# Weight-stationary matmuls taken over two weight units at a time, in a two-layer hybrid decoder trunk

## The chip, the cores and the metric

The kernel runs on one core of a Trainium2 chip. The metric is the device time of one launch in microseconds (us). Before the change it is 2441.62 us, the median of three runs (2441.19 to 2441.79). Everything below is read from one profiled execution of 2441.05 us.

## The reference, cut to what matters

The trunk has two layers on 256 tokens of width 2048, all in float32. One layer, shortened:

```
h = x @ w_in                       # 2048 -> 8336 columns: q, k, v of four head groups, and the indexer
m = concat(diff_attention x2, stick_breaking_attention, sparse_attention(indexer top-64)) @ w_out
x = layer_norm(ALPHA * x + m)
x = layer_norm(ALPHA * x + square(relu(x @ w_up)) @ w_down)     # w_up 2048 x 8192, w_down 8192 x 2048
```

Nearly all arithmetic is `activation @ weight` with 256 tokens. The sparse head group also needs a score from 16 indexer heads, summed head by head, and the 64 largest scores of each row.

## The kernel before

**Split operands.** Each float32 weight and activation is split into a rounded part (`hi`) and a remainder (`lo`), both in a reduced matmul format, and a product is the sum of hi·hi, hi·lo and lo·hi. For weights the split is made in the kernel: ScalarE (ACT) writes `hi` (line 800, `split_hi`), VectorE (DVE) writes `lo` = raw − hi (line 1048, `split_lo`).

**Chunks and units.** The weights are read in chunks of 512 output columns by 2048 rows; there are 53 a layer, numbered here from 0 in each layer: 0 the sparse group's values, 1 the indexer's keys and weights (a narrow chunk of 144 columns), 2 to 5 the indexer's queries, 6 to 16 queries, keys and values of the four groups, 17 to 20 `w_out`, 21 to 52 the MLP in four quarters of up and down chunks. A chunk consists of eight units of 256 rows, two 128-row slices each. The ring of split units (`w_hi`, `w_lo`) holds four units, so unit u of a chunk takes the place of unit u − 4, and the first four of a chunk that of units 4 to 7 of the chunk before.

**Two kinds of chunk.** In a "token" chunk the activations are TensorE's stationary operand and the weights stream by, 512 columns each (`token_tile`, lines 504 to 506). In a "feature" chunk the weights are stationary: for each of the four 128-column groups of the chunk, each with a PSUM bank of its own (n = 0 to 3), the `hi` weights meet hi and lo of the activations at once (512 columns, line 485), and the `lo` weights meet the hi activations (256 columns, line 489). There are 27 feature chunks a layer: 2 to 9, 11, 12, 14, 15, 22 to 24, and four in each of the other three quarters of the MLP.

**What sets the order.** All of it is written out by hand, and each engine runs its own list in order. TensorE (PE) waits before a unit for `lo_ready`, and before the first use of a bank in a chunk for `bank_free`. After a unit it signals `unit_free` (after the last unit `bank_full` of each bank), and `split_hi` waits for that (`before_unit` says which). ACT and DVE do their other work at fixed places between the splits: `copy_halves` and `add_halves` or `take_hidden` (the results of the chunk before) after unit 1; `index_add` (eight DVE instructions, line 1235) and, in chunk 8, `logits` after unit 6 and before unit 7; `top_k_round` after unit 7 of chunk 6 and after units 0 to 6 of chunk 7; in chunk 22 `turned_hidden_hi` (line 818) and `turned_hidden_lo` after units 6 and 7; in chunk 23 `residual_offset` (line 1135) after each unit. PE's own other work stands after a given unit too: `index_logits` after unit 1, `turn_probs`, `attend` and `turn_rows` after units 0, 2 and 4, and in chunk 22 `turn_hidden` (line 558) after units 4 and 5.

Of the kernel before, what the change touches and what calls it, by code (L numbers as in the profile page):

```python
# [23 lines left out]
PAIR = 2  # L24
# [15 lines left out]
def build(nc, x, w_in, w_out, lam_vecs, a_norm_g, b_norm_g, c_norm_g, idx_k_norm_g, idx_k_norm_b,  # L40
          ln1_g, ln1_b, w_up, w_down, ln2_g, ln2_b, rel_bias, out):
    _, SEQ, D = x.shape
# [11 lines left out]
    UNITS = KT // PAIR  # L54
    TT = SEQ // P
    HC = COLS // P
# [77 lines left out]
    with ExitStack() as ctx:  # L134
        def sb(name, shape, dt=F32):
            return ctx.enter_context(nc.sbuf_tensor(name, shape, dt))

        def sem(name):
            return ctx.enter_context(nc.semaphore(name))
# [4 lines left out]
        act_a = sb("act_a", [P, KT, 2, SEQ], F32R)  # L144
# [39 lines left out]
        pw = ctx.enter_context(nc.psum_tensor("pw", [P, HC, COLS], F32))  # L184
# [28 lines left out]
        lo_ready = sem("lo_ready")  # L213
        unit_free = sem("unit_free")
# [85 lines left out]
        def unit_home(c, u, lo):  # L300
            if CLOSING[c] and u < RING:
                return act_a[:, LOAD * u + PAIR * lo:LOAD * u + PAIR * (lo + 1)].rearrange("p k a t -> p k (a t)")
            slot = u % RING
            if OPENING[c]:
                where, slot, _ = OPEN_HOME[u]
                if where == "park":
                    return park[:, PAIR * lo:PAIR * (lo + 1)]
                if where == "act_b":
                    return act_b[:, LOAD * slot + PAIR * lo:LOAD * slot + PAIR * (lo + 1)].rearrange("p k a t -> p k (a t)")
            if c % NC == IKW:  # L310

                return w_hi[:, slot * PAIR:(slot + 1) * PAIR, lo * KW:(lo + 1) * KW]
            return (w_lo if lo else w_hi)[:, slot * PAIR:(slot + 1) * PAIR, 0:WIDTH[c]]

        def unit_hi(c, u):
            return unit_home(c, u, 0)

        def unit_lo(c, u):
            return unit_home(c, u, 1)
# [147 lines left out]
        def _(pe):  # L467

            def wait_bank(c, b):

                if USES[c][b] > 0:
                    pe.wait_ge(bank_free[b], USES[c][b])

            def feature_unit(c, u):

                hi, lo = unit_hi(c, u), unit_lo(c, u)
                pe.wait_ge(lo_ready, c * UNITS + u + 1)
                for n, b in enumerate(BANKS[c]):
                    if u == 0:

                        wait_bank(c, b)
                    cols = slice(n * P, (n + 1) * P)
                    for i in range(PAIR):
                        k = PAIR * u + i
                        nc.tensor.matmul(pw[:, b, :], hi[:, i, cols], act_a[:, k].rearrange("p a t -> p (a t)"),  # L485
                                         start=(k == 0), stop=False)
                    for i in range(PAIR):
                        k = PAIR * u + i
                        last = nc.tensor.matmul(pw[:, b, SEQ:2 * SEQ], lo[:, i, cols], act_a[:, k, 0, :],  # L489
                                                start=False, stop=(k == KT - 1))  # L490
                    if u == UNITS - 1:
                        last.then_inc(bank_full[b], 1)
                if u < UNITS - 1:
                    last.then_inc(unit_free, 1)

            def token_tile(c, u, t, src):
# [200 lines left out]
            def mixer(layer):  # L697
                for lc in range(MLP0):
# [7 lines left out]
                    for u in range(UNITS):  # L706
# [5 lines left out]
                        if KIND[c] == "feature":  # L712
                            feature_unit(c, u)
                        elif c == 0:
                            pe.wait_ge(lo_ready, u + 1)
                            for t in range(TT):
                                token_tile(c, u, t, act_a)
                                if u == 0:
                                    turn_x(0, t, 1)
                        elif lc == IKW:  # L720
                            ikw_unit(c, u)
                        else:
                            token_unit(c, u, act_a if lc < OUT0 else act_b)
# [22 lines left out]
            def mlp(layer):  # L746
                for quarter in range(QUARTERS):
                    for j in range(Q_CHUNKS):
                        c = layer * NC + MLP0 + quarter * Q_CHUNKS + j
                        if OPENING[c]:  # L750
                            open_block(c, 2 * layer + 1)
                            continue
                        if CLOSING[c]:
                            close_block(c, 2 * layer + 2)
                            continue
                        for u in range(UNITS):
                            if j < UPS:
                                feature_unit(c, u)
                                if (quarter, j) == (0, 1) and 4 <= u < 4 + TT:
                                    turn_hidden(layer, u - 4)  # L760
                                continue
                            if j == UPS:

                                pe.wait_ge(b_ready, hidden_count(layer, quarter, PAIR * u + 1))
                            token_unit(c, u, act_b)
# [797 lines left out]
```

## Time and profile before

| what | value |
|---|---|
| median of three runs | 2441.62 us |
| profiled execution | 2441.05 us, its span 2439.3 us |
| PE busy | 2419.4 us, 99% of the span |
| weight loads (PEld) busy | 2062.8 us, 85% |
| DVE busy | 1496.7 us, 61% |
| ACT busy | 1123.7 us, 46% |
| feature matmuls of 512 columns (line 485) | 3456, 33% of the chain that ended last |
| feature matmuls of 256 columns (line 489) | 3456, 16% of that chain |
| PE's share of that chain | 97% |
| mean granted clock of TensorE | 0.998 of full speed |

The first table of the page gives how long each engine was busy. Matmuls overlap their neighbours in it (a 512-column matmul is shown with 397 ns, while the next one starts some 230 ns later), so what a matmul costs is read from the distance between starts. The chain that ended last is followed back from the last instruction, at each step to what released it. Its 97% on PE says that the other engines seldom hold PE up.

### The profile page before, as it was taken

How to read it: one execution, taken by the hardware profiler on the slowest of the kernel's cores; microseconds unless marked ns; L12 is line 12 of the kernel's file. 1: busy time of each engine (PE TensorE's matmuls, PEld its weight loads, DVE VectorE, ACT ScalarE, POOL GpSimd, SP SyncE). 2: the span in 40 equal slices, each digit the busy share in tenths (PEclk: the TensorE clock that was granted, in tenths of full speed). 3: DMA queues.
4: the chain of work that ended last, by engine and by line, in shares of the span. 5: the costliest groups of instructions: out<-in, count | busy, mean ns of one | idle time of the engine just before them, and what ended most of it. 6: DMA issues, size and time to landing. Idle time of an engine off the chain costs nothing.

```text
span 2439.3 us, 30052 instructions
## 1 busy us (share of the span) xinstructions
PE 2419.4 (99%) x12557; PEld 2062.8 (85%) x12557; DVE 1496.7 (61%) x2068; ACT 1123.7 (46%) x1558; POOL 25.5 (1%) x60
## 2 busy tenths in 40 slices
PE   9999999999999999999999999999999999999998
PEld 8888888888888888888888888888888888888886
DVE  5576666667556556566675766666775655665566
ACT  4445444445345344344454444443553443443443
POOL 2000000000000000000000000000000000000001
PEclk9999999999999999999999999999999999999999
DMA  8555555646655555655555555546466565555553
GB/s 306 173 172 173 173 171 168 231 156 207 223 191 189 191 190 190 194 188 187 195 170 173 173 173 172 166 164 240 141 235 194 175 206 190 189 191 190 191 191 119
DMA packets 229752, 457.98 MB, mean 188 GB/s; under 512 B 7456, under 2 KB 12368, under 8 KB 228464
## 3 DMA queue, kind: packets, MB, share of 16 engines
q1 hardware_dynamic: 228000, 444.91, 55.6%
q0 software_dynamic: 1616, 11.14, 1.2%
q8 instruction: 99, 1.62, 0.3%
q14 instruction: 37, 0.30, 0.0%
HBM read 452.35 MB, written 3.67 MB: 187 GB/s over the span
## 4 chain that ended last, share of the span: by engine, by line
PE 97%; DVE 1%; ACT 1%; DMA 0%; issue 0%; SPq 0%; DVEq 0%; ACTq 0%
PE pw L485 33%; PE pw L489 16%; PE pw L504 14%; PE pw L506 14%; PE pw L505 14%; PE pa L583 1%; PE pa L659 1%; PE pa L580 1%; PE pa L550 0%; ACT w_hi L800 0%; PE pw L521 0%; DMA y<-in_x_dram 0%; DVE w_lo L1048 0%; PE pa L667 0%; PE pa L637 0%
## 5 line engine op out<-in xcount | busy, mean ns | idle before, releaser
L1048 DVE TENSOR_TENSOR w_lo<-raw,w_hi 128x1024 fp32r<-128x1024 f32 x804 | 971.1, 1223 | 653.0 <-ACT w_hi L800 645.4
L800 ACT ACTIVATE w_hi<-raw 128x1024 fp32r<-128x1024 f32 (+1 forms) x820 | 847.6, 1046 | 974.2 <-PE pw L506 509.2
L485 PE MATMUL pw<-act_a,w_hi 128*128 128x512 f32 x3456 | 1090.6, 397 | 3.9 <-DVE v_r L1088 3.3
L489 PEld LDWEIGHTS pw<-act_a,w_lo 128*128 128x128 f32 x3456 | 649.2, 188 | 153.2
L489 PE MATMUL pw<-act_a,w_lo 128*128 128x256 f32 x3456 | 679.2, 278 | 0.0
L485 PEld LDWEIGHTS pw<-act_a,w_hi 128*128 128x128 f32 x3456 | 528.0, 189 | 6.8 <-DVE v_r L1088 3.7
L504 PE MATMUL pw<-w_hi,act_b 128*128 128x512 f32 x1216 | 474.3, 390 | 0.1
L506 PE MATMUL pw<-w_hi,act_b 128*128 128x512 f32 x1216 | 473.2, 389 | 0.0
L505 PE MATMUL pw<-w_lo,act_b 128*128 128x512 f32 x1216 | 473.1, 389 | 0.0
L504 PEld LDWEIGHTS pw<-w_hi,act_b 128*128 128x128 f32 x1216 | 228.2, 188 | 47.7 <-DVE act_b L1331 0.9
L506 PEld LDWEIGHTS pw<-w_hi,act_b 128*128 128x128 f32 x1216 | 228.2, 188 | 47.5
L505 PEld LDWEIGHTS pw<-w_lo,act_b 128*128 128x128 f32 x1216 | 228.3, 188 | 46.7
L807 ACT ACTIVATE half<-pw 128x256 f32<-128x256 f32 x216 | 83.0, 384 | 177.4 <-PE pw L489 177.4
L504 PE MATMUL pw<-w_hi,act_a 128*128 128x512 f32 x272 | 108.7, 400 | 1.9 <-DVE w_lo L1048 1.9
L506 PE MATMUL pw<-w_hi,act_a 128*128 128x512 f32 x272 | 106.0, 390 | 0.0
L505 PE MATMUL pw<-w_lo,act_a 128*128 128x512 f32 x272 | 106.0, 390 | 0.0
L1072 DVE TENSOR_TENSOR k_t<-pw,half 128x256 f32<-128x256 f32 x120 | 50.2, 418 | 44.3 <-ACT half L807 44.3
L1109 DVE TENSOR_TENSOR y<-y,pw 128x512 f32<-128x512 f32 x48 | 33.0, 687 | 61.9 <-PE pw L506 61.9
L504 PEld LDWEIGHTS pw<-w_hi,act_a 128*128 128x128 f32 x272 | 51.1, 188 | 13.6 <-issue 3.8
L506 PEld LDWEIGHTS pw<-w_hi,act_a 128*128 128x128 f32 x272 | 51.1, 188 | 10.9
L505 PEld LDWEIGHTS pw<-w_lo,act_a 128*128 128x128 f32 x272 | 51.1, 188 | 10.5 <-issue 0.5
L1074 DVE SCALAR_TENSOR_TENSOR k_t<-k_t 128x256 f32<-128x256 f32 x120 | 51.0, 425 | 4.1
(172 smaller groups left out, 1147.8 us busy)
## 6 DMA issues: line engine op xcount, KB each, us to landing
raw<-in_w_up_dram SPq DMA_DIRECT2D x128, 1024.0 KB, 5.3
raw<-in_w_down_dram SPq DMA_DIRECT2D x128, 1024.0 KB, 5.2
raw<-in_w_in_dram SPq DMA_DIRECT2D x124, 1024.0 KB, 5.1
raw<-in_w_out_dram SPq DMA_DIRECT2D x32, 1024.0 KB, 5.1
raw<-in_w_in_dram SPq DMA_DIRECT2D x8, 512.0 KB, 10.9
work<-in_ln_g_dram POOLq DMA_DIRECT2D x4, 1024.0 KB, 6.1
work<-in_ln_b_dram POOLq DMA_DIRECT2D x4, 1024.0 KB, 8.3
raw<-in_w_in_dram SPq DMA_DIRECT2D x8, 288.0 KB, 3.9
```

The source lines that it names most:

```text
L485: nc.tensor.matmul(pw[:, b, :], hi[:, i, cols], act_a[:, k].rearrange("p a t -> p (a t)"), start=(k == 0), stop=False)
L489: last = nc.tensor.matmul(pw[:, b, SEQ:2 * SEQ], lo[:, i, cols], act_a[:, k, 0, :], start=False, stop=(k == KT - 1))
L504: nc.tensor.matmul(pw[:, b, 0:width], x_hi, hi[:, i, :], start=(k == 0), stop=False)
L505: nc.tensor.matmul(pw[:, b, 0:width], x_hi, lo[:, i, :], start=False, stop=False)
L506: last = nc.tensor.matmul(pw[:, b, 0:width], x_lo, hi[:, i, :], start=False, stop=(k == KT - 1))
L580: last = nc.tensor.matmul(pa[:, 0, h * P:(h + 1) * P], q_t[:, h, 0:P], keys(h)[:, 0:P], start=True, stop=True)
L800: nc.scalar.activation(unit_hi(c, u), raw[:, PAIR * u:PAIR * (u + 1), 0:WIDTH[c]], ACT.Copy) \
L807: nc.scalar.activation(half[:, n, :], pw[:, b, SEQ:2 * SEQ], ACT.Copy).then_inc(half_copied, 1)
L1048: V.tensor_tensor(unit_lo(c, u), raw[:, PAIR * u:PAIR * (u + 1), 0:WIDTH[c]], unit_hi(c, u).bitcast(F32), ALU.subtract).then_inc(lo_ready, 1)
L1072: V.tensor_tensor(hidden[:, n, :], pw[:, b, 0:SEQ], half[:, n, :], ALU.add).then_inc(bank_free[b], 1)
L1074: V.scalar_tensor_tensor(out=hidden[:, n, :], in0=hidden[:, n, :], scalar=0.0, in1=hidden[:, n, :], op0=ALU.max, op1=ALU.mult).then_inc(hi ...
L1109: V.tensor_tensor(piece, piece, pw[:, b, :], ALU.add).then_inc(bank_free[b], 1)
```

## The change

Only `feature_unit` changes. For odd units it returns at once; for an even unit u it waits until u and u + 1 are both split, and then runs, bank by bank, four 512-column matmuls (two slices of u, two of u + 1) and four 256-column ones. Unit u is given back after its last matmul in the last bank, unit u + 1 at the end of the pair. Work of PE that stood after an even unit now stands after the pair. No instruction is added or taken away, and the lists of ACT, DVE, SP and POOL keep their order.

```
             def feature_unit(c, u):
-                hi, lo = unit_hi(c, u), unit_lo(c, u)
-                pe.wait_ge(lo_ready, c * UNITS + u + 1)
+                if u % 2 == 1:
+                    return
+                pe.wait_ge(lo_ready, c * UNITS + u + 2)
+                pairs = [(v, i) for v in (u, u + 1) for i in range(PAIR)]
                 for n, b in enumerate(BANKS[c]):
                     if u == 0:
                         wait_bank(c, b)
                     cols = slice(n * P, (n + 1) * P)
-                    for i in range(PAIR):
-                        k = PAIR * u + i
-                        nc.tensor.matmul(pw[:, b, :], hi[:, i, cols], act_a[:, k].rearrange("p a t -> p (a t)"),
+                    for v, i in pairs:
+                        k = PAIR * v + i
+                        nc.tensor.matmul(pw[:, b, :], unit_hi(c, v)[:, i, cols], act_a[:, k].rearrange("p a t -> p (a t)"),
                                          start=(k == 0), stop=False)
-                    for i in range(PAIR):
-                        k = PAIR * u + i
-                        last = nc.tensor.matmul(pw[:, b, SEQ:2 * SEQ], lo[:, i, cols], act_a[:, k, 0, :],
+                    for v, i in pairs:
+                        k = PAIR * v + i
+                        last = nc.tensor.matmul(pw[:, b, SEQ:2 * SEQ], unit_lo(c, v)[:, i, cols], act_a[:, k, 0, :],
                                                 start=False, stop=(k == KT - 1))
-                    if u == UNITS - 1:
+                        if n == HC - 1 and v == u and i == PAIR - 1:
+                            last.then_inc(unit_free, 1)
+                    if u == UNITS - 2:
                         last.then_inc(bank_full[b], 1)
-                if u < UNITS - 1:
+                if u < UNITS - 2:
                     last.then_inc(unit_free, 1)
```

On PE, chunk 4 (indexer queries), from the last bank of unit 1 to unit 2; `pa<-k_idx_t,q_t` are the index logits. Before:

```order
L485 MATMUL pw<-act_a,w_hi 128x512 x2
L489 MATMUL pw<-act_a,w_lo 128x256 x2
L580 MATMUL pa<-k_idx_t,q_t 128x128 [waits idx_relu,bank_free3]
L580 MATMUL pa<-k_idx_t,q_t 128x128 x3
L583 MATMUL pa<-k_idx_t,q_t 128x256 x4
L485 MATMUL pw<-act_a,w_hi 128x512 [waits lo_ready]
L485 MATMUL pw<-act_a,w_hi 128x512
L489 MATMUL pw<-act_a,w_lo 128x256 x2
L485 MATMUL pw<-act_a,w_hi 128x512 x2
L489 MATMUL pw<-act_a,w_lo 128x256 x2
```

The same place in the changed kernel (its lines are two to four higher):

```order
L487 MATMUL pw<-act_a,w_hi 128x512 x3
L491 MATMUL pw<-act_a,w_lo 128x256 x4
L584 MATMUL pa<-k_idx_t,q_t 128x128 [waits idx_relu,bank_free3]
L584 MATMUL pa<-k_idx_t,q_t 128x128 x3
L587 MATMUL pa<-k_idx_t,q_t 128x256 x4
L487 MATMUL pw<-act_a,w_hi 128x512 [waits lo_ready]
L487 MATMUL pw<-act_a,w_hi 128x512 x3
L491 MATMUL pw<-act_a,w_lo 128x256 x4
L487 MATMUL pw<-act_a,w_hi 128x512 x4
L491 MATMUL pw<-act_a,w_lo 128x256 x4
```

The logits stay behind unit 1. The one wait behind them now is for units 2 and 3 together, and 32 matmuls follow before the next wait instead of 16.

On PE, chunk 22 (the second up chunk of the MLP), around the two transposes of the first chunk's rows, `pa<-ident,v_r`. Before:

```order
L489 MATMUL pw<-act_a,w_lo 128x256 x2
L558 MATMUL pa<-ident,v_r 128x128 [waits rows_relu]
L558 MATMUL pa<-ident,v_r 128x128 x3
L485 MATMUL pw<-act_a,w_hi 128x512 [waits lo_ready]
L485 MATMUL pw<-act_a,w_hi 128x512
L489 MATMUL pw<-act_a,w_lo 128x256 x2
L485 MATMUL pw<-act_a,w_hi 128x512 x2
L489 MATMUL pw<-act_a,w_lo 128x256 x2
L485 MATMUL pw<-act_a,w_hi 128x512 x2
L489 MATMUL pw<-act_a,w_lo 128x256 x2
L485 MATMUL pw<-act_a,w_hi 128x512 x2
L489 MATMUL pw<-act_a,w_lo 128x256 x2
```

And now:

```order
L491 MATMUL pw<-act_a,w_lo 128x256 x4
L562 MATMUL pa<-ident,v_r 128x128 [waits rows_relu]
L562 MATMUL pa<-ident,v_r 128x128 x3
L562 MATMUL pa<-ident,v_r 128x128 [waits rows_relu]
L562 MATMUL pa<-ident,v_r 128x128 x3
L487 MATMUL pw<-act_a,w_hi 128x512 [waits lo_ready]
L487 MATMUL pw<-act_a,w_hi 128x512 x3
L491 MATMUL pw<-act_a,w_lo 128x256 x4
```

The first transpose moved from behind unit 4 to behind unit 5, and both stand together ahead of the last pair.

## Rows read from the trace of the kernel before

**Rows 1.** Timeline, PE, steady stretch of chunk 23: start us, us, engine, line, operation, count.
```profile
563.36 0.63 PE L485 MATMUL pw<-act_a,w_hi 128*128 128x512 f32 x2
563.83 0.39 PE L489 MATMUL pw<-act_a,w_lo 128*128 128x256 f32 x2
...
568.93 0.63 PE L485 MATMUL pw<-act_a,w_hi 128*128 128x512 f32 x2
```

**Rows 2.** Timeline, PE, a token chunk; 21 matmuls lie between these two starts.
```profile
1000.39 0.39 PE L504 MATMUL pw<-w_hi,act_b 128*128 128x512 f32 x1
...
1005.15 0.39 PE L504 MATMUL pw<-w_hi,act_b 128*128 128x512 f32 x1
```

**Rows 3.** Timeline, PE, chunk 1 (narrow); 8 matmuls lie between these two starts.
```profile
40.12 0.34 PE L521 MATMUL pw<-w_hi,act_a 128*128 128x288 f32 x1
...
41.09 0.34 PE L521 MATMUL pw<-w_hi,act_a 128*128 128x288 f32 x1
```

**Rows 4.** Timeline, PE, chunk 6: starts of units 3, 4 and 6.
```profile
152.63 0.63 PE L485 MATMUL pw<-act_a,w_hi 128*128 128x512 f32 x2
...
155.42 0.63 PE L485 MATMUL pw<-act_a,w_hi 128*128 128x512 f32 x2
...
160.99 0.63 PE L485 MATMUL pw<-act_a,w_hi 128*128 128x512 f32 x2
```

**Rows 5.** Timeline, ACT, chunk 6: split_hi of unit 6; in brackets idle before, and releaser.
```profile
152.89 1.06 ACT L800 ACTIVATE w_hi<-raw 128x1024 fp32r<-128x1024 f32 x1 [1.82 <-PE pw L489]
```

**Rows 6.** Timeline, DVE: index_add and split_lo of unit 7, chunk 6; unit 3, chunk 7.
```profile
155.13 3.59 DVE L1235 SCALAR_TENSOR_TENSOR score<-work,ikw,score 128x128 f32<-128x128 f32 x8
158.76 1.23 DVE L1048 TENSOR_TENSOR w_lo<-raw,w_hi 128x1024 fp32r<-128x1024 f32 x1
...
171.53 1.23 DVE L1048 TENSOR_TENSOR w_lo<-raw,w_hi 128x1024 fp32r<-128x1024 f32 x1
```

**Rows 7.** Timeline, PE: chunk 22's start, its fourth bank, transpose; chunk 23's start.
```profile
532.83 0.61 PE L485 MATMUL pw<-act_a,w_hi 128*128 128x512 f32 x2
...
536.73 0.73 PE L485 MATMUL pw<-act_a,w_hi 128*128 128x512 f32 x2 [1.65 <-DVE v_r L1088]
...
548.68 0.60 PE L558 MATMUL pa<-ident,v_r 128*128 128x128 f32 x4
...
558.17 0.70 PE L485 MATMUL pw<-act_a,w_hi 128*128 128x512 f32 x2
```

**Rows 8.** Timeline, DVE: unit 7 of chunk 22; chunk 23's first take-up and unit 3.
```profile
550.90 1.22 DVE L1048 TENSOR_TENSOR w_lo<-raw,w_hi 128x1024 fp32r<-128x1024 f32 x1 [0.26 <-ACT w_hi L800]
...
557.61 0.41 DVE L1072 TENSOR_TENSOR k_t<-pw,half 128x256 f32<-128x256 f32 x1
...
564.05 1.22 DVE L1048 TENSOR_TENSOR w_lo<-raw,w_hi 128x1024 fp32r<-128x1024 f32 x1
```

**Rows 9.** Timeline, ACT, chunk 22: split_hi of unit 7, behind the transposed rows.
```profile
549.81 1.05 ACT L800 ACTIVATE w_hi<-raw 128x1024 fp32r<-128x1024 f32 x1
```

**Rows 10.** Timeline, DVE, first layer: units 0 and 1 of chunk 2.
```profile
42.20 2.36 DVE L1048 TENSOR_TENSOR w_lo<-raw,w_hi 128x1024 fp32r<-128x1024 f32 x2 [1.19 <-ACT w_hi L800]
```

**Rows 11.** Timeline, PE: chunk 2's start, first layer; its third bank, second layer.
```profile
43.77 0.67 PE L485 MATMUL pw<-act_a,w_hi 128*128 128x512 f32 x2
...
1254.90 0.74 PE L485 MATMUL pw<-act_a,w_hi 128*128 128x512 f32 x2 [0.41 <-DVE ikw L1199]
```

**Rows 12.** Timeline, PE: the start of chunk 24.
```profile
580.78 0.63 PE L485 MATMUL pw<-act_a,w_hi 128*128 128x512 f32 x2
```

**Rows 13.** Timeline, DVE: units 2 to 5 of chunk 24.
```profile
584.00 4.87 DVE L1048 TENSOR_TENSOR w_lo<-raw,w_hi 128x1024 fp32r<-128x1024 f32 x4
```

**Rows 14.** Windows: from, to, us, busy of each engine (count), PEclk, DMA share, GB/s.
```profile
534.00:537.00 3.00, 1.35 (x8) 1.06 (x7) 2.57 (x4) 0.10 (x1) 0.00 (x0) 1.00 0.74 255
```

**Rows 15.** Timeline, PE: the warming matmuls at the kernel's start.
```profile
1.13 4.13 PE L769 MATMUL pa<-ones 128*128 128x128 f32 x18 [1.13 <-DVE ones L1518]
...
6.18 2.17 PE L769 MATMUL pa<-ones 128*128 128x128 f32 x18
```

## The prediction, made before the changed kernel had run

> **What bounds the kernel now.** I read the busy shares first (PE 99%, DVE 61%), then the chain that ended last (97% PE), then PE's timeline chunk by chunk, and for each feature chunk when the lo part of a unit was ready against when PE started that unit. The kernel is bound by PE's stream of matmuls; other engines hold it up in a few places only. So two questions decide the change: does the new order make the stream denser, and are the weights still split in time?
>
> **The matmuls themselves.** Before, four matmuls (512, 512, 256, 256 columns) come round every (568.93 − 563.36) / 8 = 0.696 us [rows 1]: the two wide ones take 0.47 us from start to start, 0.233 each, the two narrow ones the remaining 0.23, 0.115 each. A unit is 4 banks of this, 2.79 us, a pair 5.57. In a token chunk, where all are 512 wide, one takes (1005.15 − 1000.39) / 21 = 0.227 us [rows 2]. At the granted 2.4 GHz 512 columns are 0.213 us, so a matmul costs 0.013 us over its columns there; four at that rate would be 1536 columns, 0.640 + 4 × 0.0134 = 0.694 us. Only 0.003 us of 0.696 is left that switching between widths could cost. The change halves the switches in 54 chunks × 16 groups of eight: at most 0.003 × 864 = 2.3 us gained. On the other side a longer run of narrow matmuls could be held by the weight loads: the nearest row is the narrow chunk, (41.09 − 40.12) / 8 = 0.121 us for each load and its matmul [rows 3], and four of those with four at 0.227 make 1.392 a group, as now. I take 1 us gained, between 2.3 gained and, for records I may misread by 0.002 a group, 2 lost.
>
> A rule bears on how far single steps can be trusted: the Trainium skill (Perfetto Trace Analysis, section "Per-instruction lifecycle: what the profiler-reported window actually captures") says that a matmul's reported start is the start of its operand prefetch, and its end an estimate. By it 0.233 and 0.115 are no separate prices and only their sum counts, which is how I use them; who takes them as prices gets the first rival below.
>
> **What the pair does to the splits.** Two things, both against the kernel. PE now needs the odd unit when it starts the even one, 2.79 us sooner. And the even unit is given back two 256-column matmuls before the pair's end instead of one unit earlier: later by 2.79 − 0.23 = 2.56 us. The unit four places on is split later by as much, and the odd one behind it in DVE's list too, if DVE has work between them. Such an odd unit loses 2.79 + 2.56 = 5.35 us of slack. Where nothing lies between, it is enough: the split of a pair takes about 3.7 us from its release (0.26 until ACT starts, as between 152.63 and 152.89 [rows 4, 5], hi 1.06, lo twice 1.23) and PE has 5.57. The cover is gone in these places.
>
> *Chunks 3, 4, 5, 6 (index_add) and 8 (logits), in both layers.* In chunk 6 unit 2 ended at 152.63, hi of unit 6 started at 152.89 [rows 4, 5], index_add ran from 155.13 for 3.59 us, and lo of unit 7 ended at 158.76 + 1.23 = 159.99 [rows 6]; PE wanted it at 163.78, so 3.79 us remained. After: 159.99 + 2.56 = 162.55, and 0.05 until PE starts; PE wants units 6 and 7 at the end of unit 5, 160.99 [rows 4]. Stall 1.61 us. A matmul group behind a wait takes 0.10 us longer (0.73 against 0.63 in the x2 rows [rows 1, 7]): 1.71. The other four look the same to 0.02 us; in chunk 8 the logits' three instructions stand in for index_add. 5 × 1.71 = 8.55 us a layer. ACT is not what binds: index_relu ends before unit 6 is split.
>
> *Chunk 7.* DVE does a top-k round after each split, so a unit takes 2.57 us and nothing catches up. The chain is tied to the last bank of chunk 6, i.e. to the start of chunk 7 (160.99 + 5.58 = 166.57), in both orders. Lo of unit 3 ended at 171.53 + 1.23 = 172.76 [rows 6], 6.19 in; the pair wants it at 5.57. Stall 0.62 + 0.05 + 0.10 = 0.77 us. Later units of it have over 0.4 us left.
>
> *Chunk 2.* Its start now waits for unit 1 as well: lo ended at 42.20 + 2.36 = 44.56 [rows 10], PE had started at 43.77 [rows 11]: + 0.84 with the 0.05. But four waits for banks in its unit 0 go, since each bank is now asked for 1.39 us apart: 0.29 us in the first layer and 0.89 in the second, whose largest is the wait for ikw (0.41 shown idle, more with the slow group behind [rows 11]). Net + 0.55 and − 0.05.
>
> *Chunk 22.* The fourth bank was asked for at 2.09 us and came at 536.73 − 532.83 = 3.90 [rows 7]; now it is asked for at 4.18, so the 1.82 us stall goes and 0.10 with it; the wait of 0.24 at its end goes too. What is late next is unit 7: ACT first takes the transposed rows, which PE now makes after unit 5, not 4. The transpose starts at 6 × 2.79 = 16.72; lo of unit 7 ended 550.90 + 1.22 − 548.68 = 3.44 after it [rows 7, 8], with hi of unit 7 at + 1.13 [rows 9]. So 20.16, PE at 20.21, the pair ends at 20.21 + 0.10 + 5.57 = 25.88. Before, the chunk took 558.17 − 532.83 = 25.34 [rows 7]: + 0.54. PE idles 2.7 us there.
>
> *Chunk 23.* DVE's residual_offset stands after each split. From lo of unit 7 of chunk 22 (20.16) it does 0.6 + 1.1 + 0.6 + 1.1 + 0.6 us and starts the take-up at 24.2; from there to the end of unit 3 it is 564.05 + 1.22 − 557.61 = 7.66 [rows 8], so 31.84, or 5.96 into the chunk against 5.57 wanted: stall 0.39 + 0.15. The old bank waits of this chunk, 0.32, go: + 0.2.
>
> *Other up chunks (22 boundaries to check).* Chunk 24 starts at 580.78 [rows 12]; lo of units 2 and 3 ended at 584.00 + 4.87 / 2 = 586.44 [rows 13], 5.66 in, where 5.57 is wanted. But the hidden rows' take-up was late because DVE needs 0.80 us a bank and banks filled every 0.70; now they fill every 1.39, and the last one's chain ends 0.3 us sooner: 5.3 to 5.4. I count no stall; if I am wrong by 0.2 on the 21 to 22 such places it costs 4 us.
>
> **Sum.** First layer 8.55 + 0.77 + 0.55 + 0.54 + 0.2 = 10.6, second 10.0, the stream − 1: + 19.6 us on the profiled execution's 2441.05, 2460.7; the median of the runs is 0.57 above that execution, so 2461.2.
>
> **Rivals.** (a) *The stream gets denser and pays for it.* If wide matmuls among their own kind run at the token chunk's 0.227 [rows 2], while the narrow ones keep 0.115 [rows 1], a group of eight takes 1.368 instead of 1.393: 864 × 0.025 = 21.6 us, and the time is 2439, a little faster than before. For it: the wide steps do read 0.233 next to narrow ones. Against: it needs a matmul to cost 0.013 over its columns when wide and 0.008 when narrow, and the narrow chunk's 0.121 a load [rows 3] speaks for slower, not faster. It decides once the gain passes 20.6 us.
> (b) *The narrow run is held by its loads on top:* narrow steps of 0.121 with wide ones left at 0.233, 864 × 4 × 0.006 = 21 us more, 2482. The same two rows, read the other way.
> (c) *Half of the stalls are not there*, since DVE's or ACT's lists slip less than I count (another release, an earlier hi): 2451.
> (d) *The clock falls in the new pauses.* At the start 18 small matmuls took 4.13 us, later 2.17 [rows 15]: the lower level (1.2 GHz) for about that stretch costs 2 us. With 16 pauses that is up to 32 us, 2493. The stretch with the 1.65 us pause kept 1.00 granted [rows 14], and only chunk 22's pause is longer. The Trainium skill (TensorE: Matmul & The Clock Gate, section "HAM oscillation — how this bites in real kernels") says that pauses between bursts can bring the engine back to half clock; no row before the change shows it, and I give it little: if at chunk 22 alone, 4 us more.
>
> **Chances.** Forecast 0.77, (a) 0.06, (b) 0.04, (c) 0.08, (d) 0.05. The likeliest time is 2461, its own range 2456 to 2467 (the up chunks' 4 us, the stream's 2.3 and − 2, 0.2 a stall). The range for 8 in 10 is 2453 to 2468. A change of 0.2%, 4.9 us, is about what a measurement can tell from none: slower 0.93; (a) splits into 0.03 faster and 0.04 same, with a sliver of (c).
>
> **What would show it.** In the profile after, PE should wait for DVE w_lo at the start of the fourth pair of chunks 3 to 6 and 8 by about 1.5 us idle each, ten times, at the second pair of chunk 7 by 0.5, and at the fourth of chunk 22 by 2.5; the wait for v_r should be gone. Four wide and four narrow matmuls should come round every 1.39 us. If that reads 1.37, (a) is right; 1.41, (b); if the waits for w_lo come to less than 10 us, my account of the splits is wrong.

## The result and the profile after

| | before | after |
|---|---|---|
| median of the runs | 2441.68 us | 2470.98 us (2470.77 to 2472.13) |
| ratio of the runs | | 1.0122, 95% interval 1.011 to 1.0134 |
| span of the profiled execution | 2439.3 us | 2470.3 us |
| mean granted clock of TensorE | 0.998 | 0.997 |

The change costs 29.3 us in the medians, 31.0 from profile to profile (the profiled execution after, 2472.13 us, is the slowest of its runs). Forecast were 2461 and a range of 2453 to 2468: the direction was right, the size 10 us short, and the time lies outside the range.

The page after: the span, the busy times, and the engines' shares of the chain that ended last.

```profile
span 2470.3 us, 30052 instructions
...
PE 2432.3 (98%) x12557; PEld 2073.7 (84%) x12557; DVE 1485.4 (60%) x2068; ACT 1103.1 (45%) x1558; POOL 25.5 (1%) x60
...
PE 93%; DVE 4%; ACT 2%; issue 1%; DMA 0%; DVEq 0%; ACTq 0%
```

PE left 4 points of the chain to DVE and ACT. Its busy time rose by 13 us for the same 12557 matmuls, so waits are not all of it. PE's waits, as engine, line, what released it, total us, times, longest:

```profile
PE pw L487 <- DVE w_lo L1052: 21.5, 18, 2.5
```

Of line 485 before, the page had waits for `v_r`, 3.3 us in two, and for `ikw`, 0.4 in one. Both are gone and 18 waits for split weights stand in their place: five by 1.39 us in each layer (chunks 3 to 6 and 8), 0.69 at chunk 2, 0.48 in chunk 7, 2.45 in chunk 22, 0.18 in chunk 23. Here is the first kind on PE's timeline, chunk 4's last pair, and behind it DVE's list over the same stretch:

```profile
113.47 0.64 PE L491 MATMUL pw<-act_a,w_lo 128*128 128x256 f32 x4
115.49 1.19 PE L487 MATMUL pw<-act_a,w_hi 128*128 128x512 f32 x4 [1.39 <-DVE w_lo L1052]
```

```profile
109.45 1.23 DVE L1052 TENSOR_TENSOR w_lo<-raw,w_hi 128x1024 fp32r<-128x1024 f32 x1 [5.86 <-ACT w_hi L804]
110.59 3.59 DVE L1239 SCALAR_TENSOR_TENSOR score<-work,ikw,score 128x128 f32<-128x128 f32 x8
114.22 3.50 DVE L1052 TENSOR_TENSOR w_lo<-raw,w_hi 128x1024 fp32r<-128x1024 f32 x3
```

Unit 6 is split, then the eight instructions of index_add run, and only then comes unit 7, done at 114.22 + 1.23 = 115.45. PE had been free since 114.1 and starts at 115.49. The 5.86 us ahead of unit 6 are DVE's wait for a unit that PE now gives back late. Before, it was 4.24 us:

```profile
104.16 1.23 DVE L1048 TENSOR_TENSOR w_lo<-raw,w_hi 128x1024 fp32r<-128x1024 f32 x1 [4.24 <-ACT w_hi L800]
```

That is 12.33 us into chunk 4 (which then started at 91.83), and now it is 14.95 us in (94.50): later by 2.62, where the prediction has 2.56.

The steady stream, chunk 24 [rows 1]:

```profile
597.19 1.09 PE L487 MATMUL pw<-act_a,w_hi 128*128 128x512 f32 x4
...
599.99 1.09 PE L487 MATMUL pw<-act_a,w_hi 128*128 128x512 f32 x4
600.92 0.64 PE L491 MATMUL pw<-act_a,w_lo 128*128 128x256 f32 x4
601.40 1.09 PE L487 MATMUL pw<-act_a,w_hi 128*128 128x512 f32 x4
...
605.61 1.09 PE L487 MATMUL pw<-act_a,w_hi 128*128 128x512 f32 x4
```

Six groups of eight lie between the first start and the last: (605.61 − 597.19) / 6 = 1.403 us, where two groups of four took 1.393.

Chunk 22, from its two transposes to the last pair [rows 7], then windows over it (from, to, us, busy of each engine with count, granted clock, DMA share, GB/s) [rows 14]:

```profile
560.93 1.03 PE L562 MATMUL pa<-ident,v_r 128*128 128x128 f32 x8
564.42 2.08 PE L487 MATMUL pw<-act_a,w_hi 128*128 128x512 f32 x4 [2.45 <-DVE w_lo L1052]
566.30 1.05 PE L491 MATMUL pw<-act_a,w_lo 128*128 128x256 f32 x4
```

```profile
562.00:564.00 2.00, 0.00 (x0) 0.00 (x0) 1.55 (x2) 2.00 (x4) 0.00 (x0) 1.00 0.00 0
564.00:566.00 2.00, 1.58 (x4) 1.29 (x5) 2.00 (x3) 1.49 (x2) 0.00 (x0) 0.51 0.27 44
566.00:568.00 2.00, 2.00 (x10) 1.77 (x9) 2.00 (x4) 0.39 (x1) 0.00 (x0) 0.64 0.95 307
568.00:570.00 2.00, 2.00 (x14) 1.79 (x13) 1.85 (x5) 0.39 (x1) 0.00 (x0) 1.00 0.95 278
```

Behind the pause the first four wide matmuls take 2.08 us instead of 1.09: the clock is at its lower level (1.2 of 2.4 GHz) for about 3.4 us (2.0 in the window at 0.51 and 1.4 in the one at 0.64), and the last pair takes 7.07 us until chunk 23 starts, where pair_two_two, below, takes 5.69 at full clock. The second layer does the same, with 7.26 us. That makes 2.9 us.

### The profile page after: what moved, and what is told of

It reads as the page before. It is cut to its first block, busy times and chain, and to the rows that moved or that the text cites. A ratio compares the mean times of both kernels' runs of the same rounds, so it can differ in the third digit from the quotient of the medians.

```text
span 2470.3 us, 30052 instructions
## 1 busy us (share of the span) xinstructions
PE 2432.3 (98%) x12557; PEld 2073.7 (84%) x12557; DVE 1485.4 (60%) x2068; ACT 1103.1 (45%) x1558; POOL 25.5 (1%) x60
## 4 chain that ended last, share of the span: by engine, by line
PE 93%; DVE 4%; ACT 2%; issue 1%; DMA 0%; DVEq 0%; ACTq 0%
PE pw L487 31%; PE pw L491 15%; PE pw L508 14%; PE pw L510 14%; PE pw L509 14%; DVE w_lo L1052 2%; DVE score L1239 1%; ACT w_hi L804 1%; PE pa L587 1%; PE pa L663 1%; PE pa L584 1%; PE pa L554 0%; PE pw L525 0%; PE pa L671 0%; PE pa L641 0%
## 5 line engine op out<-in xcount | busy, mean ns | idle before, releaser
L804 ACT ACTIVATE w_hi<-raw 128x1024 fp32r<-128x1024 f32 (+1 forms) x820 | 834.9, 1043 | 1058.0 <-PE pw L491 540.5
L487 PE MATMUL pw<-act_a,w_hi 128*128 128x512 f32 x3456 | 950.5, 397 | 21.5 <-DVE w_lo L1052 21.5
L487 PEld LDWEIGHTS pw<-act_a,w_hi 128*128 128x128 f32 x3456 | 593.6, 189 | 105.7 <-DVE w_lo L1052 25.2
L491 PEld LDWEIGHTS pw<-act_a,w_lo 128*128 128x128 f32 x3456 | 530.9, 189 | 73.9
L491 PE MATMUL pw<-act_a,w_lo 128*128 128x256 f32 x3456 | 550.3, 281 | 0.0
L510 PEld LDWEIGHTS pw<-w_hi,act_a 128*128 128x128 f32 x272 | 51.1, 188 | 10.9
## 6 DMA issues: line engine op xcount, KB each, us to landing
raw<-in_w_in_dram SPq DMA_DIRECT2D x8, 512.0 KB, 10.9
```

Of the source, the lines that this page charges most:

```text
L487: nc.tensor.matmul(pw[:, b, :], unit_hi(c, v)[:, i, cols], act_a[:, k].rearrange("p a t -> p (a t)"), start=(k == 0), stop=False)
L491: last = nc.tensor.matmul(pw[:, b, SEQ:2 * SEQ], unit_lo(c, v)[:, i, cols], act_a[:, k, 0, :], start=False, stop=(k == KT - 1))
L510: last = nc.tensor.matmul(pw[:, b, 0:width], x_lo, hi[:, i, :], start=False, stop=(k == KT - 1))
L804: nc.scalar.activation(unit_hi(c, u), raw[:, PAIR * u:PAIR * (u + 1), 0:WIDTH[c]], ACT.Copy) \
```

## The experiments

Open after the result: whether the 1.403 comes from the runs of four or from the pairs; whether sooner need and later release explain the waits; what the pause in chunk 22 costs. On the stream I held two theories against each other: N, a narrow matmul (256 columns) costs more straight behind another narrow one than behind a wide one (512 columns); and R, runs of four of one width cost more than runs of two. The expectations quoted below give each its numbers.

**alt_single and alt_pair.** Wide and narrow alternate one by one; in the kernel before, and inside the pairs of the changed one.

```
                     for i in range(PAIR):
                         ...                            # wide matmul of slice i
-                    for i in range(PAIR):
-                        k = PAIR * u + i
                         last = ...                     # narrow matmul of slice i
```

> The kernel before, unit by unit, but inside a bank the order is wide, narrow, wide, narrow (512, 256, 512, 256 columns). Theory N (a narrow matmul straight behind a narrow one costs about 0.009 us more than one behind a wide one; this explains 0.697 us per four before and 1.402 us per eight after): the four now take 0.688 us, 1728 times 0.009 = 15 us less, so about 2426 us. Rival S (every switch of width costs): four switches instead of two, 0.699 us or more per four, 2445 us or more. Rival F (fixed prices, the pair's slower rate comes from something else): 0.697 us, 2442 us.

> The changed kernel, pairs of units, but wide and narrow alternate slice by slice. Theory N: eight take 1.376 us instead of 1.402, 864 times 0.026 = 22 us less than the changed kernel, with the same waits for w_lo (they grow a little, as PE runs ahead faster): about 2450 us. Rival S: 1.41 us per eight or more, 2475 us or more. Rival F: 2471 us.

Measured: alt_single 2452.18 us, ratio 1.0045 (1.003 to 1.006); alt_pair 2470.80, 1.012 (1.0105 to 1.0135). PE's timeline of alt_single:

```profile
589.85 0.39 PE L485 MATMUL pw<-act_a,w_hi 128*128 128x512 f32 x1
...
591.93 0.39 PE L485 MATMUL pw<-act_a,w_hi 128*128 128x512 f32 x1
...
938.21 0.40 PE L485 MATMUL pw<-act_a,w_hi 128*128 128x512 f32 x1
...
940.33 0.40 PE L485 MATMUL pw<-act_a,w_hi 128*128 128x512 f32 x1
```

Six couples of a wide and a narrow matmul lie between the first two rows, and six between the last two: 2.08 and 2.12 us, or 0.693 and 0.707 us per four. The list of instructions is the same; the stream has two rates, and jumps between them only where something interrupts it (a transpose, a wait). Of 338 undisturbed units in this trace 57 run at the one and 281 at the other, and in alt_pair some 47 and 264. The better one beats every other order seen here, the worse one is the worst.

alt_single adds no wait and loses 10.9 us; the mean over its units, 0.7045 against 0.6977, gives 0.0068 × 1728 = 11.8. So the order of widths counts at an equal number of matmuls. The 0.688 that theory N gave isn't there: the better rate comes near it, but most units run at the worse one, above the kernel before. And one rate for one length of run, as theory R has it, is too simple as well. Rival S's numbers came for alt_single (0.699 us or more, 2445 us or more), but S can't be the rule: the changed kernel and snake, below, have fewer switches than the kernel before and a slower stream. In alt_pair, with 16.7 us of waits in 17 places where the changed kernel has 21.5 in 18, alternating makes no difference to the changed kernel's time; a slower stream waits less, so this time alone says little about the order.

**early_need.** The kernel before, but an even unit waits for the odd one too.

```
-                pe.wait_ge(lo_ready, c * UNITS + u + 1)
+                if u % 2 == 0:
+                    pe.wait_ge(lo_ready, c * UNITS + u + 2)
```

> The kernel before with its own order of matmuls and its own releases; only the wait moves: before an even unit PE waits for that unit and the next. Theory of the splits: no wait in chunks 3 to 6 and 8 (3.8 us of slack less 2.8), waits at the start of chunk 2 (0.8), at unit 2 of chunk 7 (0.7), of chunk 23 (1.3) and some 0.1 at the other up chunks: about 4 us a layer, 2450 us. Rival (needing the odd unit early is the whole cost): 16 us or more, 2458 us or more.

2450.34 us (2450.22 to 2450.84), 1.0038 (1.0023 to 1.0052), with

```profile
PE pw L486 <- DVE w_lo L1049: 4.6, 6, 1.1
PE pw L486 <- DVE v_r L1089: 3.3, 2, 1.7
```

As expected: needing the odd unit 2.79 us sooner costs 9.1 us alone. In each layer it is 0.8 us in chunk 7, 1.4 in chunk 23, 0.85 at the start of chunk 2 (of which its unit 0 gives back 0.2 and 0.8), and 0.18 to 0.20 in each of ten other up chunks. These last are the places where the prediction worked out 5.66 against 5.57 wanted and then counted nothing, since with pairs the banks fill more slowly; here they fill as before, and the wait is there. None of the ten waits of 1.39 us is there. The wait for `v_r` stays, since the banks are still asked for 0.7 us apart.

**late_release.** early_need, and units are given back as late as the pair does.

```
+                    if u % 2 == 1 and n == HC - 1:     # behind its last wide matmul, for u - 1
+                        last.then_inc(unit_free, 1)
-                if u < UNITS - 1:
+                if u % 2 == 1 and u < UNITS - 1:
                     last.then_inc(unit_free, 1)
```

> As early_need, and the even unit is given back only two narrow matmuls before the end of the odd one, as in the changed kernel; the order of matmuls is that of the kernel before. Theory of the splits: waits of 1.6 us at unit 6 of chunks 3 to 6 and 8 come on top (8.5 us a layer), the stream keeps 0.697 us per four: about 25 us over before, 2466 us, and no drop of the clock in chunk 22. Rival (the lost time of the changed kernel is mostly in the stream of matmuls): under 2455 us.

2494.07 us (2492.81 to 2496.37), 1.0217 (1.0202 to 1.0232): 28 us over what I expected, a miss, and I had expected no drop of the clock. Its waits, and the costliest place with a window behind it:

```profile
PE pw L486 <- DVE w_lo L1051: 18.9, 16, 1.4
PE pa L670 <- DVE work L1326: 16.9, 6, 3.9
```

```profile
241.56 0.40 PE L492 MATMUL pw<-act_a,w_lo 128*128 128x256 f32 x2
245.88 1.97 PE L670 MATMUL pa<-ident,work 128*128 128x128 f32 x8 [3.93 <-DVE work L1326]
```

```profile
246.00:252.00 6.00, 6.00 (x23) 5.34 (x24) 1.62 (x2) 0.00 (x0) 0.00 (x0) 0.54 0.54 173
```

The ten waits came when the later release was added to the sooner need, which is what the run was for; the later release by itself was not run. What I had not seen is line 670: in chunks 9, 11 and 14 PE transposes attention rows after unit 4, in the middle of a pair. In the paired kernel they move behind unit 5, 2.8 us later; here they stay, while DVE's list, which must split the later-freed units first, has slipped. The transposes wait up to 3.9 us, and the clock falls behind five of the six pauses (0.54 over 6 us here). The pauses are 16.9 us, and some 24 us at the lower level in this trace are worth up to 12 more, which together is about the 28. The changed kernel's profile has no such wait; that its later transposes are the reason fits, but no run tests it.

**pair_two_two.** The changed kernel, but two wide, two narrow of unit u, then the same of u + 1, in each bank.

```
-                    for v, i in pairs:   # four wide
-                    for v, i in pairs:   # four narrow
+                    for v in (u, u + 1):
+                        for i in range(PAIR):   # two wide
+                        for i in range(PAIR):   # two narrow
```

> The changed kernel with its waits and releases kept, but inside a bank the order of the kernel before: two wide and two narrow matmuls of unit u, then two and two of unit u + 1. Theory R (the slower stream of the changed kernel comes from four of one width in a row): eight take 1.394 us instead of 1.403, 864 times 0.0096 = 8 us less than the changed kernel, about 2463 us, with the waits for w_lo and the drop of the clock in chunk 22 unchanged. Rival B (it comes from eight matmuls in a row into one bank): 1.403 us, 2471 us.

2464.51 us (2461.93 to 2465.23), 1.0092 (1.0077 to 1.0107); span 2460.1. PE's timeline:

```profile
597.12 0.63 PE L488 MATMUL pw<-act_a,w_hi 128*128 128x512 f32 x2
...
599.21 0.63 PE L488 MATMUL pw<-act_a,w_hi 128*128 128x512 f32 x2
```

Three groups of four in 2.09 us: 0.697, the old rate, as theory R has it. Rival B, eight matmuls in a row into one bank, is out. The profiled execution shows the same pause in chunk 22, and behind it the clock stays up:

```profile
563.06 0.73 PE L488 MATMUL pw<-act_a,w_hi 128*128 128x512 f32 x2 [2.45 <-DVE w_lo L1053]
```

```profile
562.00:564.00 2.00, 0.94 (x5) 0.85 (x6) 2.00 (x3) 2.00 (x3) 0.00 (x0) 1.00 0.00 0
564.00:566.00 2.00, 2.00 (x14) 1.74 (x13) 2.00 (x3) 0.52 (x2) 0.00 (x0) 1.00 0.84 220
```

This one execution isolates the waits: same pairs, old rate, full clock, span + 20.8 us. It is the fastest of the four; the other three have a mean clock of 0.997 or 0.998 where it has 0.999, so the clock probably fell in them.

**snake.** The kernel before, but in every second bank (not of unit 0) the narrow two go first, so four of one width meet across two banks.

```
+                    if u > 0 and n % 2 == 1:
+                        # narrow, narrow, wide, wide
```

> The kernel before unit by unit, with its waits; from unit 1 on the second and fourth bank take their two narrow matmuls first, so that four of one width stand in a row across banks. Theory R: 0.701 us per four instead of 0.697, 1512 times 0.0045 = 7 us more, about 2448 us. Rival K (what costs is which slices follow each other, not how many of a width): 0.697 us, 2442 us.

2448.56 us (2448.17 to 2448.83), 1.0029 (1.0018 to 1.004).

```profile
589.38 1.09 PE L489 MATMUL pw<-act_a,w_hi 128*128 128x512 f32 x4
...
592.19 1.09 PE L489 MATMUL pw<-act_a,w_hi 128*128 128x512 f32 x4
```

Two groups of eight in 2.81 us, 1.405 each; over all undisturbed units of the trace it is 0.701 per four. Runs of four without pairs and without a new wait cost 7.2 us: the stream's term by itself, with the sign that I had wrong, and the 0.701 per four and 2448 us of theory R.

**long_runs**, one execution. A unit's eight wide matmuls over all banks, then its eight narrow ones.

```
                     for i in range(PAIR):   # wide
+                for n, b in enumerate(BANKS[c]):
                     for i in range(PAIR):   # narrow
```

> The kernel before unit by unit, but in a unit all eight wide matmuls come first, bank after bank, then all eight narrow ones. Only the steady rate is read from it, since the banks fill closer together and the take-up of the results then holds PE up at the start of chunks. Theory R (runs of one width cost more the longer they are): above 1.403 us per eight, 2.81 us or more a unit. Rival (the loss comes at run length four only, a matter of how starts fall on the engine's clock): at or below 1.394 us per eight, 2.79 us a unit.

2499.63 us. Most of what it loses are waits for banks at the starts of chunks, since all four are asked for in unit 0's first run; the granted clock also fell in chunk 22 of both layers, behind pauses of 2.38 us. The rate is read in steady state:

```profile
602.04 2.00 PE L485 MATMUL pw<-act_a,w_hi 128*128 128x512 f32 x8
603.88 1.11 PE L491 MATMUL pw<-act_a,w_lo 128*128 128x256 f32 x8
604.83 2.00 PE L485 MATMUL pw<-act_a,w_hi 128*128 128x512 f32 x8
```

A unit takes 604.83 − 602.04 = 2.79 us, 0.698 per four, between the two expectations, and below the 0.701 of runs of four: that runs cost more the longer they are is refuted. The steps inside settle at 0.227 us for a wide matmul, the token chunk's [rows 2], and 0.120 for a narrow one.

**adds_behind_7.** The changed kernel with index_add, and the logits of chunk 8, behind the split of unit 7.

```
-                        if IDX0 < lc <= IDX0 + IDX_CHUNKS and u == 6:
+                        if IDX0 < lc <= IDX0 + IDX_CHUNKS and u == 7:
                             index_add(layer, lc - 1 - IDX0)
-                                if (lc, u) == (v, 6):
+                                if (lc, u) == (v, 7 if kind == "C" else 6):
                                     logits(layer, g, 1)
```

> The changed kernel, but on DVE index_add and the sparse group's second logits stand behind the split of unit 7 instead of unit 6. Theory of the splits: the ten waits of 1.6 us at the fourth pair of chunks 3 to 6 and 8 go (17 us), and the wait in chunk 7 grows from 0.6 to about 2 us, since DVE's chain of top-k rounds starts as late as before against a chunk that comes sooner: about 14 us less, 2457 us. Rival (these waits hide others): under 5 us less.

2466.97 us (2464.52 to 2468.02), 1.0106 (1.0089 to 1.0122): 4 us better than the changed kernel, 10 us worse than expected. Its waits, and the longest new one:

```profile
PE pw L487 <- DVE q_t L1063: 8.8, 4, 3.0
PE pw L487 <- DVE w_lo L1052: 7.1, 8, 2.5
```

```profile
220.87 1.16 PE L487 MATMUL pw<-act_a,w_hi 128*128 128x512 f32 x4 [3.03 <-DVE q_t L1063]
```

The ten waits behind index_add are gone, which confirms their cause. But DVE's work went to where the banks are emptied: chunks 7 and 9 now wait for a bank (`q_t` is its take-up), by 1.35 and 3.03 us, and behind the longer one the clock fell in the second layer (0.51 from 1441 to 1444 us) and not in the first (1.00 from 222 to 226). The expectation took for free a place that I had not followed to its next consumer.

**turn_early and two_two_early.** The changed kernel, and pair_two_two, with the transposes of chunk 22 two units earlier.

```
-                                if (quarter, j) == (0, 1) and 4 <= u < 4 + TT:
-                                    turn_hidden(layer, u - 4)
+                                if (quarter, j) == (0, 1) and 2 <= u < 2 + TT:
+                                    turn_hidden(layer, u - 2)
```

> The changed kernel, but both transposes of chunk 22 stand behind its second pair instead of its third. Theory: the pause of 2.7 us before the last pair goes, and with it the stretch at a granted clock near 0.5 behind it (1.4 to 1.6 us in each layer): 8 us less, 2462.5 us, mean clock 0.999. Rival (the clock falls for another reason, or the pause only moves to chunk 23): 5.4 us less or fewer, 2465.5 us or more.

> The changed kernel with both repairs: inside a bank two wide, two narrow, unit by unit, and both transposes of chunk 22 behind its second pair. What is left are the waits for split weights. If the parts add up: stream 8 us, pause and clock of chunk 22 some 6 us less than the changed kernel, 2457 us, with runs within 0.5 us of each other, since no pause is long enough for the clock to fall. Rival (the clock falls in the pauses of 1.6 us as well, in some runs): runs 1 us or more apart.

turn_early 2465.34 us (2465.27 to 2465.42), 1.0097 (1.0082 to 1.0113); two_two_early 2458.26 (2458.10 to 2458.60), 1.007 (1.0054 to 1.0085). The pause in chunk 22 and the lower clock behind it are gone, 5.6 us against the changed kernel, 3 less than I expected. Between the profiles chunk 22 is 4.1 and 4.3 us shorter, the 8 us that I had counted. 1.5 of them came back in the next chunk, where the wait before the second pair rose from 0.18 to 0.92 us in each layer; and the changed kernel's profiled execution, from which I had counted, is 1.15 us slower than its median.

```profile
574.18 1.21 PE L487 MATMUL pw<-act_a,w_hi 128*128 128x512 f32 x4 [0.92 <-DVE w_lo L1052]
```

turn_early to two_two_early is 7.1 us, and 6.8 between their profiles: the stream's term once more. The spread went with the pause: 0.15 and 0.5 us between runs, against 1.4 and 3.3 with it.

**pairs_in_22.** The kernel before, with pairs in chunk 22 alone, for its first two and last two units, two wide and two narrow at a time.

```
+                if c % NC == MLP0 + 1 and u in (0, 1, UNITS-2, UNITS-1):
+                    if u % 2 == 0:
+                        paired_units(c, u)       # as in pair_two_two
+                    return
```

> The kernel before, and only in chunk 22 units 0 and 1 and units 6 and 7 are taken as pairs, in the order two wide, two narrow. The stall of 1.9 us at the fourth bank of chunk 22 and the bank waits of 0.24 at its end and 0.32 at the start of chunk 23 go, in both layers: 4 to 5 us less than before, 2437 us. Rival (units 6 and 7 come too late as a pair, 3.03 us of slack less 2.79, or chunk 23 waits for its split weights instead): 2 us less or fewer, 2439.5 us or more.

2437.42 us (2437.16 to 2437.74), 0.9984 (0.9976 to 0.9993). It is below both kernels, by 3.7 us where I expected 4 to 5; that is less than the 0.2% that I called measurable, but the interval leaves 1 out. PE's timeline at the chunk's first unit, and its fourth bank:

```profile
533.25 0.62 PE L483 MATMUL pw<-act_a,w_hi 128*128 128x512 f32 x2
...
537.42 0.62 PE L483 MATMUL pw<-act_a,w_hi 128*128 128x512 f32 x2
...
556.67 0.70 PE L511 MATMUL pw<-act_a,w_hi 128*128 128x512 f32 x2
```

The fourth bank is asked for 4.17 us in, without a wait, where PE had stood 1.65 us [rows 7]. The chunk takes 23.42 us instead of 25.34, and twice 1.92 is the whole gain. Chunk 23 takes 22.61 us as before, so the bank waits of 0.32 us that I expected to go are still there.

## Why the prediction was wrong, step by step

Durations of chunks in us, start to start, in the first layer. pair_two_two has the waits of the changed kernel, but the old rate of the stream and full clock; what it adds is to be held against the prediction's waits.

| chunks | before | pair_two_two | after | added by the waits: predicted, measured |
|---|---|---|---|---|
| 3 to 6, 8 | 24.91 | 26.61 to 26.64 | 26.68 to 26.73 | 1.71, 1.70 to 1.72 |
| 7 | 22.29 | 23.06 | 23.19 | 0.77, 0.77 |
| 22 | 25.34 | 25.89 | 27.37 | 0.54, 0.55 |
| 23 | 22.61 | 22.80 | 22.89 | 0.2, 0.19 |
| other up chunks | 22.29 | 22.29 | 22.45 | 0, 0 |

**The splits: right.** Chunk 2 started 0.85 later behind chunk 1, against 0.84, and lost 0.17 and 0.78 us of its bank waits in the two layers, where 0.29 and 0.89 were to go. In chunk 6 of the changed kernel the last pair started 20.98 us in, where 20.95 follows from [rows 4 to 6]. That no other up chunk would stall held too: lo of unit 3 is ready 5.30 us in, as guessed. In all, pair_two_two's + 20.8 us stands against 20.6. That the sooner need is not the whole cost is shown by early_need (+ 9.1, and none of the ten waits) and by late_release, where the later release on top brings the ten waits. That index_add, and in chunk 8 the logits, on DVE are what lies between is shown by adds_behind_7.

**The stream: the step that failed.** The prediction took 1 us gained, between 2.3 gained and 2 lost. Measured: 1.403 instead of 1.393 us a group of eight. That is 0.16 us in an up chunk without a wait, and 0.06 to 0.10 in chunks 3 to 6, 8, 11 and 14; added up over the chunks of the changed kernel and of pair_two_two it is 6.9 us lost. In medians it is 7.2 (snake against before), 7.1 (turn_early against two_two_early) and 6.5 (the changed kernel against pair_two_two). I had argued that only a switch between widths could cost something and that there are fewer of them. What the runs show, in steady state:

| length of a run of one width | us per four matmuls |
|---|---|
| 1 (alt_single, alt_pair) | 0.707, in a sixth of the units 0.693 |
| 2 (before, pair_two_two) | 0.697 |
| 4 (after, snake) | 0.702, 0.701 |
| 8 (long_runs) | 0.698 |

Steps inside one group of the changed kernel are 235, 233, 236, 224 ns wide and 118, 120, 120, 120 narrow; the next group is 5 ns shorter. Over both, a narrow step is 118.6 ns on average, where before it was 115.3, and a wide one 232.3, where it was 233. So the narrow ones moved towards the 0.121 us per load of [rows 3], as rival (b) had it, but by 0.003 and not 0.006, and the wide ones gave a little back. These are distances between reported starts; only the sum of a group is a price.

With the steps at which long_runs settles, 0.227 and 0.120, four would take 0.694, as the prediction had it, and the kernel before is 0.003 over that, as it said. What it took for granted is that this loss is one price for each switch, whatever the length of the runs. It isn't: over these settled steps one wide and one narrow run together cost 0.003 us more in runs of two, 0.016 in runs of four and 0.017 in runs of eight. Half as many runs at five to six times the loss is what the change bought, and at eight the same loss is spread over twice the matmuls. The narrow chunk says something on the 0.120. Its matmuls have 288 and 144 columns in turn:

```profile
40.30 0.23 PE L522 MATMUL pw<-w_hi,act_a 128*128 128x144 f32 x1
```

That is 216 columns on average at 0.121 us, and a long run of 256 columns settles at 0.120. So there the columns don't set the price, which fits a price per load and doesn't prove it.

The bound of + 2 us was drawn from how well I could read a row, not from the nearest row that spoke against me; with the narrow chunk's rate as the upper end it would have been + 21, and the range would have held the time. Why two is cheaper than four, and why the alternating order has two rates, stays open: no run separates loads from matmuls. The Trainium skill (TensorE: Matmul & The Clock Gate, section "Wait — 56ns, not 53.3ns?") gives a fixed 2.5 ns over the columns' time for each matmul at the upper level; by it 512 columns would take 0.216 us and the order of widths would not count, while these traces settle at 0.227 and have an order that counts.

**The clock: rival (d) in its small form.** It was given 0.05 and priced at 4 us "if at chunk 22 alone"; it came there alone, for 2.9 us in the profiled execution. turn_early took pause, lower clock and spread away together. By this trace the Trainium skill (TensorE: Matmul & The Clock Gate, section "HAM oscillation — how this bites in real kernels") is right that pauses between bursts can bring half clock. But it isn't certain from run to run: behind the same 2.45 us pause pair_two_two's profile keeps 1.00. The 1.39 us pauses never brought it down.

**The sum.** Waits 20.8, stream 6.9, clock 2.9: 30.6 of the 31.0 us between the two profiles. The prediction had 19.6. Of the 11.4 us that were missing there, 7.9 are the stream's term (6.9 lost instead of 1 gained) and 2.9 the clock's, which stood in no term of the sum. Between the medians 10 are missing, as the other runs of the changed kernel are about 1 us faster than the profiled one. The direction of the forecast was no luck, since the waits carry it. The stream's miss alone puts the time at 2469, outside the range; the clock's alone would have left it inside, at 2464. Rival (a), a denser stream that would have made the kernel faster, is refuted by the 1.403; rival (c), half of the stalls, by 18 waits that are all there, 21.5 us.

What isn't settled: what sets the stream's rate for a given order, what the later release costs by itself, and what decides whether the clock falls behind a given pause.

## What to carry to other kernels

Taking ring slots in pairs costs slack twice, once by the sooner need and once by the later release, and with work between two splits both add up on the odd unit; count it per place, as here, and it comes out to some tenths of a microsecond. Bound an unknown rate by the nearest row that speaks against you, however well the steady rows can be read: a few nanoseconds times thousands of matmuls were most of the error. Use a reordering only where its wait is, as the pairs in one chunk of 53 show, and follow each piece of work that you move to the next engine that waits for it.

## What the runs showed of the hardware

- The cost of a mixed stream of matmuls of 512 and 256 columns depends on how they are grouped: 0.707, 0.697, 0.701 to 0.702 and 0.698 us per four in runs of one, two, four and eight. In runs of one the same instructions also came at 0.693, unit after unit, until an interruption moved the stream to the other rate: a steady rate read in one place needn't hold in the next. A long run settles at 0.227 and 0.120 us each.
- Whether the granted clock fell to its lower level behind a pause was not a matter of the pause's length alone. Behind the 2.45 us idle in chunk 22 (2.73 between the starts of the matmuls around it) it fell in both layers of the changed kernel and of alt_pair, in the first layer alone in adds_behind_7, and in neither in pair_two_two, each in one execution. Behind 3.03 us it fell once of two times, behind 2.38 (long_runs) both times, behind 2.26 (late_release) three times of four, and behind 1.39 or 1.65 never. Where it fell in the changed kernel, some 3.4 us at half clock cost 1.4 and 1.6 us. A pause of 3.9 us was followed by 0.54 over 6 us.
- The kernels with such pauses are spread more widely: 1.4 to 4.0 us between runs of after, pair_two_two, adds_behind_7, late_release and alt_pair, and 0.15 to 0.7 in turn_early, two_two_early, early_need, snake and pairs_in_22. It is a hint and no proof: alt_single, without such a pause but with two rates of its stream, has 2.5, and one series of the kernel before had 1.4.
